# RWKV's inputs as a stream of their own in a three-mixer transformer block: separate generator, two input buffers, one PSUM bank, new interleaving tables

## The reference, cut to what matters

```python
y_a = hgrn2_mixer(a_q, a_ff, a_fb, a_i, lbs[l], ...) * jax.nn.silu(a_g)
y_b = retention_mixer(b_q, b_k, b_v, ...) * jax.nn.silu(b_g)
y_c = rwkv7_mixer(c_s, rwkv_mu[l], ...) * jax.nn.silu(c_g)
gates = jax.nn.sigmoid(merge.reshape(b, t, 3, D_MODEL))
mixed = (gates[:, :, 0] * (y_a @ w_branch_a[l]) + gates[:, :, 1] * (y_b @ w_branch_b[l])
         + gates[:, :, 2] * (y_c @ w_branch_c[l]))
x = x + (mixed @ w_out[l])
```

## Time and profile before

| What | Value |
|---|---|
| timed executions | 3178.53, 3178.54, 3192.47 us |
| the profiled execution | 3192.13 us, its span 3190.3 us |
| mean granted TensorE clock | 0.974 |
| TensorE busy | 3027.6 us, 95% of the span |
| VectorE / ScalarE / GpSimd busy | 52% / 22% / 8% |
| DMA queues, share of 16 engines | 33.2% weights, 3.3% the inverse's traffic |
| mixers of layer 0 | 31 to 1015.3 us |
| mixers of layer 1 | 1052 to 2031.6 us |

### The profile page before, as it was taken

One profiled execution on the slowest core, in us unless ns is written; L12 is line 12 of the kernel. 1 busy time (PEld: TensorE's weight loads), 2 busy tenths in 40 slices (PEclk: granted clock), 3 DMA queues, 4 the chain that ended last, 5 costly groups with the idle time before them and its releaser, 6 DMA issues.

```text
span 3190.3 us, 45074 instructions
## 1 busy us (share of the span) xinstructions
PE 3027.6 (95%) x18944; PEld 2516.2 (79%) x18944; DVE 1655.0 (52%) x3430; ACT 686.4 (22%) x1327; POOL 260.1 (8%) x326
## 2 busy tenths in 40 slices
PE   8989998889999998999799999899999999999999
PEld 7878877778887787888687888698677959866794
DVE  3556645456221464664645531176325757646575
ACT  3223423233110232342324211110111001013100
POOL 1201212012000020221102100000000000000000
PEclk9989989999999999999899999999999999999999
DMA  5323332233334332323223433445344544532453
GB/s 215 108 75 121 91 95 102 63 109 116 114 96 162 132 109 69 128 87 98 92 94 91 135 115 112 154 151 169 123 152 146 169 164 158 171 130 107 146 172 119
DMA packets 153753, 395.55 MB, mean 124 GB/s; under 512 B 90288, under 2 KB 106800, under 8 KB 109648
## 3 DMA queue, kind: packets, MB, share of 16 engines
q1 hardware_dynamic: 51376, 367.94, 33.2%
q10 hardware_dynamic: 100608, 19.93, 3.3%
q0 software_dynamic: 1568, 4.79, 0.4%
HBM read 380.04 MB, written 12.59 MB: 123 GB/s over the span
## 4 chain that ended last, share of the span: by engine, by line
PE 85%; DVE 7%; DMA 4%; ACT 1%; issue 1%; ACTq 1%; POOL 0%; DVEq 0%; SPq 0%
PE bank L414 27%; PE bank L1943 17%; PE bank L1961 7%; PE bank L431 6%; PE bank L1766 6%; PE bank L1829 3%; PE bank L1369 2%; PE bank L1972 1%; DMA rw_ex<-xT_scratch 1%; PE bank L749 1%; DMA xT_scratch<-rw_bm 1%; PE bank L768 1%; DVE rw_ex L680 1%; PE bank L916 1%; PE bank L1652 1%
## 5 line engine op out<-in xcount | busy, mean ns | idle before, releaser
L414 PE MATMUL bank<-h_features,weight_ring 128*128 128x256 f32 x4192 | 969.5, 388 | 9.9 <-DMA weight_ring<-in_w_in 4.9
L414 PEld LDWEIGHTS bank<-h_features,weight_ring 128*128 128x128 f32 x4192 | 799.4, 194 | 125.0 <-issue 5.1
L431 PE MATMUL bank<-weight_ring,h_features 128*128 128x256 f32 (+1 forms) x896 | 205.3, 379 | 0.6 <-ACT rt_qk L1670 0.6
L431 PEld LDWEIGHTS bank<-weight_ring,h_features 128*128 128x128 f32 x896 | 164.1, 190 | 24.8 <-issue 2.3
L1943 PE MATMUL bank<-h_features,weight_ring 128*128 128x128 f32 x1408 | 172.0, 275 | 6.1 <-DVE h_features L527 6.1
L1943 PEld LDWEIGHTS bank<-h_features,weight_ring 128*128 128x128 f32 x1408 | 164.3, 192 | 6.9 <-DVE h_features L527 6.9
L2014 ACT COPY mem_normed<-bank 128x128 f32<-128x128 f32 x88 | 23.5, 267 | 481.7 <-PE bank L1943 481.7
L1766 PE MATMUL bank<-y_features,weight_ring 128*128 128x256 f32 x512 | 120.7, 386 | 0.0
L1766 PEld LDWEIGHTS bank<-y_features,weight_ring 128*128 128x128 f32 x512 | 96.1, 192 | 13.4 <-issue 0.7
L2099 DVE TENSOR_TENSOR mem_normed<-mem_normed,bank 128x256 f32<-128x256 f32 x88 | 37.1, 421 | 130.8 <-PE bank L1943 130.8
L1943 PE MATMUL bank<-h_features,y_hgrn_features 128*128 128x128 f32 x704 | 93.0, 275 | 0.0
(11 more groups left out here) (544 smaller groups left out, 4925.1 us busy)
## 6 DMA issues: line engine op xcount, KB each, us to landing
weight_ring<-in_w_in SPq DMA_DIRECT2D x146, 1024.0 KB, 4.9
weight_ring<-in_f00w SPq DMA_DIRECT2D x33, 1024.0 KB, 4.8
weight_ring<-in_f01w SPq DMA_DIRECT2D x33, 1024.0 KB, 4.9
weight_ring<-in_f10w SPq DMA_DIRECT2D x33, 1024.0 KB, 4.9
weight_ring<-in_f11w SPq DMA_DIRECT2D x33, 1024.0 KB, 4.8
weight_ring<-in_w_b SPq DMA_DIRECT2D x16, 1024.0 KB, 4.9
weight_ring<-in_w_out SPq DMA_DIRECT2D x16, 1024.0 KB, 4.9
weight_ring<-in_conv_in SPq DMA_DIRECT2D x10, 1024.0 KB, 4.9
```

The source lines that it names most:

```text
L414: m = e.matmul(bank[:, j, :], w[:, k, j * P:(j + 1) * P], x[:, k, :], start=k == 0, stop=k == kt - 1, skip_group_check=True)
L431: m = e.matmul(bank[:, t * n:(t + 1) * n], x[:, k, t * P:(t + 1) * P], w[:, k, :], start=k == 0, stop=k == kt - 1, skip_group_check=True)
```

## The change

Five things change together.

1. RWKV's inputs (`c_r, c_k, c_v, c_g`, the `kk` norm, the transposes of `v`, the gate) leave the generators `rwkv_*` and become generators `rwkv_inputs_*`, a fourth letter P in the strings. `r, k, v, kk, vt` exist twice, so P of quarter q waits only for the end of quarter q - 2.
2. RWKV's four banks are divided: bank 3 alone for P, bank 0 for `rhs`, banks 1 and 2 for the rest of RWKV.
3. The gates of all three mixers are kept where the mixer's output will stand (`g.yc3`, `g.ya3`, `g.yT3`); `finish_dve` computes in another tile and multiplies into it. This frees three gate tiles.
4. The semaphore of the inverse is divided: one pair for the inverse (`x`), one for its transpose (`xT`), and the first doubling waits for `x` alone.
5. All the interleaving strings of the mixers are new, and equal for both layers.

```diff
 ("mixers0", "tensor"):
-    "H2 R20 H2 R5 H11 R4 H R6 H6 B6 H B3 R H2 R5 B R2 H2 R B R B R2 H2 R4 B2 R2 B R2 H2 R B R B R2 H2 R6 B3 "
+    "R P4 R4 H P4 H2 P4 H2 P5 H P H P H5 P H P4 H3 R2 P R2 P R2 P R4 P H6 B P4 B R H R3 P R2 P R2 P R P2 R H2 "
 ("mixers0", "sync"):
-    "H R4 H4 B6 H5 R4 B6 H5 B5 R4 B H B H B H B H B H B3 R4 B4 H2 B H B2 H B H B H B H2 B R8 ",
+    "P H P2 H P H2 P2 H B P2 B P B4 H4 B H P B P2 B4 P H5 B5 P B P3 B6 H2 B H2 B4 H B8 H9 R9 ",
...
-    R.r, R.k, R.v, R.kk, R.bonus = (R(n, *for_t) for n in ("r", "k", "v", "kk", "bonus"))
-    R.vt, R.o = R("vt", TT, 2 * P), R("o", TT, 2 * P)
-    R.gate = R("gate", *for_t)
+    R.inputs = [[R(f"{n}{i}", *for_t) for n in ("r", "k", "v", "kk")] + [R(f"vt{i}", TT, 2 * P)] for i in range(2)]
...
-    R.prod, R.x, R.xT = (... for z in (R.sig, R.bm, R.ex))
+    R.prod, R.x, R.xT = (... for z in (R.sig, R.ex, R.bm))
...
         if lv == BLOCK:
-            e.wait_ge(g.rw_inverse_sem, 64 * ((4 * l + q) * 2 + d + 1))
+            e.wait_ge(g.rw_x_sem, 32 * ((4 * l + q) * 2 + d + 1))
...
+            e.wait_ge(g.rw_xT_sem, 32 * ((4 * l + q) * 2 + d + 1))
...
+def rwkv_inputs_pe(e, g, l, q):
+    S = g.ri
+    _, _, v, _, vt = g.R.inputs[q % 2]
+    for name in ("c_r", "c_k", "c_v", "c_g"):
+        yield from features_pe(e, g, S, g.hT3, f"{name}{q}", l)
+    yield
+    bank = pairs(g.banks.take(S, "kkn", l, q))
+    ...
+def rwkv_inputs_act(e, g, l, q):
+    ...
+    if q >= 2:
+        e.wait_ge(*g.rw.dve.at("end", l, q - 2))
+    elif l:
+        e.wait_ge(*g.rw.dve.at("merged", l - 1, 3))
...
-    bank = g.banks.take(S, "rhs", *W)
+    bank = g.banks.take(g.rh, "rhs", *W)
...
-        e.tensor_tensor(y, y, gate[:, n0:n0 + 2, :], ALU.mult)
+        e.tensor_tensor(y, z, y, ALU.mult)
...
-        self.rw, self.hg = Stream(self, "rwkv", (0, 1, 2, 3)), Stream(self, "hgrn", (4, 5))
+        self.rw, self.hg = Stream(self, "rwkv", (1, 2)), Stream(self, "hgrn", (4, 5))
+        self.rh = Stream(self, "rwkv_rhs", (0,))
+        self.ri = Stream(self, "rwkv_inputs", (3,))
```

More of the change, by code:

```diff
@@ L771, in doublings_pe, with rwkv_inputs_sp @@
         yield
-def rwkv_sp(e, g, l):
+def rwkv_inputs_sp(e, g, l, q):
+    for name in ("c_r", "c_k", "c_v", "c_g"):
+        w_in_load(e, g, l, f"{name}{q}")
+        yield
+def rwkv_inputs_pe(e, g, l, q):
+    S = g.ri
+    _, _, v, _, vt = g.R.inputs[q % 2]
+    for name in ("c_r", "c_k", "c_v", "c_g"):
+        yield from features_pe(e, g, S, g.hT3, f"{name}{q}", l)
+    yield
+    bank = pairs(g.banks.take(S, "kkn", l, q))
+    for free in g.banks.free("kkn", l, q):
+        e.wait_ge(*free)
+    e.wait_ge(*S.dve.at("kk2", l, q))
+    for j in range(2):
+        m = e.matmul(bank[:, j, :], g.const("block_ones"), view(flat(vt), (2, T))[:, j, :], start=True, stop=True,
+                     skip_group_check=True)
+    m.then_inc(*S.pe.up("kkn", l, q))
+    for t in range(TT):
+        yield
+        if t == 0:
+            e.wait_ge(*S.dve.at(f"c_v{q}", l))
+        bank = g.banks.take(S, "vt", l, q, t)
+        for free in g.banks.free("vt", l, q, t):
+            e.wait_ge(*free)
+        for n in range(2):
+            m = e.transpose(bank[:, n * P:(n + 1) * P], v[:, n, t * P:(t + 1) * P], g.const("eye"))
+        m.then_inc(*S.pe.up("vt", l, q, t))
+    yield
@@ new lines, in rwkv_inputs_act @@
+def rwkv_inputs_act(e, g, l, q):
+    S = g.ri
+    pe, dve, act = S.pe, S.dve, S.act
+    r, k, v, _, vt = g.R.inputs[q % 2]
+    yield
+    if q >= 2:
+        e.wait_ge(*g.rw.dve.at("end", l, q - 2))
+    elif l:
+        e.wait_ge(*g.rw.dve.at("merged", l - 1, 3))
+    if q == 0:
+        e.wait_ge(*g.st.dve.at("mu", l))
+    for name, out, tile0 in (("c_r", r, 0), ("c_k", k, 8), ("c_v", v, 16)):
+        shifted_act(e, g, S, out, tile0 + 2 * q, f"{name}{q}", l)
+        yield
+    e.wait_ge(*pe.at(f"c_g{q}", l))
+    e.activation(g.yc3[:, 2 * q:2 * q + 2, :], pairs(g.banks.get(f"c_g{q}", l)), ACT.Sigmoid).then_inc(
+        *act.up(f"c_g{q}", l))
+    yield
+    e.wait_ge(*dve.at("kkv", l, q))
+    e.activation(vt, vt, ACT.Sqrt).then_inc(*act.up("kks", l, q))
+    for t in range(TT):
+        yield
+        e.wait_ge(*pe.at("vt", l, q, t))
+        e.wait_ge(*dve.at("kk", l, q))
+        e.copy(vt[:, t, :], g.banks.get("vt", l, q, t)[:, 0:2 * P]).then_inc(*act.up("vt", l, q, t))
+        g.banks.empty(act, "vt", l, q, t)
+    yield
@@ new lines, in rwkv_inputs_dve @@
+def rwkv_inputs_dve(e, g, l, q):
+    S = g.ri
+    pe, dve, act = S.pe, S.dve, S.act
+    r, k, v, kk, vt = g.R.inputs[q % 2]
+    norm = view(flat(vt), (2, T))
+    for name, out, tile0 in (("c_r", r, 0), ("c_k", k, 8), ("c_v", v, 16)):
+        yield
+        shifted_dve(e, g, S, out, tile0 + 2 * q, l, f"{name}{q}", l)
+        if name == "c_k":
+            yield
+            e.wait_ge(*dve.now())
+            for n in range(2):
+                z = e.tensor_scalar(kk[:, n, :], k[:, n, :], g.col(f"k_k{l}", 2 * q + n), None, ALU.mult)
+            z.then_inc(*dve.up())
+            e.wait_ge(*dve.now())
+            e.tensor_tensor(norm, kk, kk, ALU.mult).then_inc(*dve.up("kk2", l, q))
+    yield
+    gate = g.yc3[:, 2 * q:2 * q + 2, :]
+    e.wait_ge(*act.at(f"c_g{q}", l))
+    e.tensor_tensor(gate, gate, pairs(g.banks.get(f"c_g{q}", l)), ALU.mult).then_inc(*dve.up(f"c_g{q}", l))
+    g.banks.empty(dve, f"c_g{q}", l)
+    yield
+    e.wait_ge(*pe.at("kkn", l, q))
+    e.tensor_scalar(norm, pairs(g.banks.get("kkn", l, q)), 1.0, 1e-12, ALU.mult, ALU.add).then_inc(
+        *dve.up("kkv", l, q))
+    g.banks.empty(dve, "kkn", l, q)
+    yield
+    e.wait_ge(*act.at("kks", l, q))
+    e.reciprocal(norm, norm).then_inc(*dve.up())
+    e.wait_ge(*dve.now())
+    e.tensor_tensor(kk, kk, norm, ALU.mult).then_inc(*dve.up("kk", l, q))
+    yield
@@ L775, in rwkv_sp, with quarters @@
+def quarters(program, e, g, l):
     for q in range(4):
-        for name in ("c_r", "c_k", "c_v", "c_g"):
-            w_in_load(e, g, l, f"{name}{q}")
-            yield
+        yield from program(e, g, l, q)
 def rwkv_pe(e, g, l):
@@ L785, in rwkv_pe @@
     for q in range(4):
-        for name in ("c_r", "c_k", "c_v", "c_g"):
-            yield from features_pe(e, g, S, g.hT3, f"{name}{q}", l)
[L789 to L792, removed]
-            bank = g.banks.take(S, "vt", l, q, t)
-            for free in g.banks.free("vt", l, q, t):
-                e.wait_ge(*free)
-            for n in range(2):
-                m = e.transpose(bank[:, n * P:(n + 1) * P], R.v[:, n, t * P:(t + 1) * P], eye)
-            m.then_inc(*pe.up("vt", l, q, t))
-        yield
-        yield
-        bank = pairs(g.banks.take(S, "kkn", l, q))
-        for free in g.banks.free("kkn", l, q):
-            e.wait_ge(*free)
-        e.wait_ge(*dve.at("kk2", l, q))
-        for j in range(2):
-            m = e.matmul(bank[:, j, :], ones, R.ex[:, j, :], start=True, stop=True, skip_group_check=True)
-        m.then_inc(*pe.up("kkn", l, q))
+        _, _, _, _, vt = R.inputs[q % 2]
         for d in range(2):
@@ L1109, in rwkv_dve @@
     for q in range(4):
[L1110 to L1131 removed]
+        r, k, v_, kk, _ = R.inputs[q % 2]
         for d in range(2):
@@ L1268, in center_dve, with finish_dve @@
     yield
-def finish_dve(e, g, S, branch, yT, n_tiles, t0, gain, shift, bonus, gate, l, q):
+def finish_dve(e, g, S, yT, tmp, n_tiles, t0, gain, shift, bonus, l, q):
     dve = S.dve
@@ L1659, in retention_act @@
-def retention_act(e, g, l):
+    for name in ("b_q", "b_k"):
+        yield from features_pe(e, g, S, g.hT3, f"{name}{q}", l)
+    for s in range(2):
+        yield
+        bank = pairs(g.banks.take(S, "rot", l, q, s))
+        for free in g.banks.free("rot", l, q, s):
+            e.wait_ge(*free)
+        e.wait_ge(*act.at(("b_q", "b_k")[s], l, q))
+        for j in range(2):
+            m = e.matmul(bank[:, j, :], g.const("rot"), (B.q, B.k)[s][:, j, :], start=True, stop=True,
+                         skip_group_check=True)
+        m.then_inc(*pe.up("rot", l, q, s))
+        yield from tokens_pe(e, g, S, g.hT3, f"b_v{q}{s}", l)
@@ new lines, in retention_pe @@
+    for s in range(2):
+        yield from features_pe(e, g, S, g.hT3, f"b_g{q}{s}", l)
+    for h in range(2):
+        yield
+        bank = pairs(g.banks.take(S, "score", l, q, h))
+        for free in g.banks.free("score", l, q, h):
+            e.wait_ge(*free)
+        e.wait_ge(*dve.at("rot", l, q, 1))
+        for j in range(TT):
+            m = e.matmul(bank[:, j, :], B.k[:, h, j * P:(j + 1) * P], B.q[:, h, :], start=True, stop=True,
+                         skip_group_check=True)
+        m.then_inc(*pe.up("score", l, q, h))
+        yield
+        bank = g.banks.take(S, "mix", l, q, h).rearrange("p (t v) -> p t v", t=TT)
+        for free in g.banks.free("mix", l, q, h):
+            e.wait_ge(*free)
+        e.wait_ge(*dve.at("score", l, q, h))
+        e.wait_ge(*act.at(f"b_v{q}1", l))
+        for t in range(TT):
+            for j in range(TT):
```

(15 more changed lines are left out.)

323 lines of the change are left out of this document (120 added, 203 removed), and 96 rows, old and new, of the table ORDER.

## The result

The changed kernel takes 3091.1 us (median of four; 3085.3 to 3099.1), the kernel before, timed beside it, 3180.8 us. The ratio is 0.973, its 95% interval 0.970 to 0.976. The forecast was 3089, with a range of 3040 to 3145. The profiled execution took 3096.9 us, its span is 3095.1.

The account below looks back on a forecast made before the run. TensorE, busy 95%, bounds the kernel; only its mixers' idle time (111.0 us) and lower clock can be won. Idle 48 + 9 + 15 - 5 - 4 = 63 plus clock 27, together 90 off 3178.5, gives 3089; range 3040 to 3145.

Parts of the forecast that it names:

- HGRN: TensorE's waits at HGRN's finish, last mask and scale products: 55.8 us, of which 48 saved by cover, bounds 35 and 54.
- The inverse: TensorE's waits for loads of RWKV's block inverse: 18.8 us, 9 saved, bounds 0 and 17; need 28 to 32, cover 26 to 31.
- Ring, kk norm, bonus: TensorE's small waits for weight ring, kk norm and bonus: of some 19 us, 15 saved, bounds 8 and 18.
- P's bank: TensorE waiting for DVE's shift to read P's single bank: 5 us added for both layers, bounds 0 and 30.
- Score banks: RWKV's scores with two banks where they had four: about 1 us in a few of 16 units, 4 us added.
- Table loads: ScalarE's 25 added loads, 32 us, mostly paid beside other work; if all in TensorE's chains, 3121, chance 0.03.
- The clock: TensorE's lower clock in the mixers, real cost put at 47 us, follows the waits: 27 us saved.
- A: Rival: mixer waits move rather than go; about 40 us of idle saved, nothing of the clock: 3139, chance 0.20.
- B: Rival: nearly all mixer idle goes, 10 us per layer stay; 122 us saved, 3057, at the outside 3030; chance 0.16.
- C: Rival: slower, TensorE waits at P's single bank, 56 turns; 3256 at 3 us per turn, 3211 at 2.2; chance 0.07.
- D: Rival: cover does not matter, the streams' ends only meet elsewhere and the layer's time stays: 3178, chance 0.05.
- my case: Likeliest case: mixer waits mostly covered, 90 us saved, 3089 (3075 to 3120), chance 0.52.

Follow-up runs that it names:

- the old order: Changed kernel's structure with the orders of the kernel before: 3344.6 us, 1.052 of the kernel before; the same with two banks for P: 3239.2 us, 1.018.
- the run made for it: Changed kernel with the square root of the kk norm replaced by a plain copy, 14 table loads fewer: 3085.6 us, 0.970 of the kernel before.
- the control: Changed kernel run again, unedited, on the chip of the runs beside it: 3082.5 us, 0.970 of the kernel before.
- the loads held: Changed kernel with four weight loads per layer waiting on SyncE until the inverse has landed: 3049.4 us, 0.959; same edit in the kernel before: 3151.7 us, 0.992.

## Why the prediction was right, and where it was not

*HGRN: 48 us saved forecast, 52.6 came.* Right, and for the reason given. The same waits return with the old order (51.7 us), and return in part when the cover alone is taken away (24.6 us at six finishes). The chain, said to need 5.6 us, costs 4.1 in the mean when uncovered (up to 6.3), with its norm ahead of RWKV's work. The 2 us set aside for quarter 1 did not come.

*The inverse: 9 saved forecast, none came* (18.8 to 19.1). This is the step that failed. It read "need 28 to 32 us, cover 26 to 31" and took the need as the inverse's own, from landings of 2.5 and 3.6 us. Those medians of the kernel before hid what the other queue does, and they did not carry over: the stores' became 5.0 and 5.4 under the new order. The need grows with the weight chunks that move beside the transfers, up to 10.5 us and more for a load that takes 3.2 alone. The division was priced at about 1 us a unit; it was worth some 30 us in all, but only by making good part of this. I had looked at SyncE for the ring's sake alone, whether a chunk comes too late, and not for what its burst hits. The evidence stood in the kernel before too, in stores of up to 6.2 and loads of up to 7.1 us within the mixers.

*Ring, kk norm, bonus: 15 forecast.* None of the three has a row now. Over the run they had come to 4.9, 4.1 and 7.0, which is 16.0.

*P's bank: 5 forecast, 0.6 came.* Its price per turn was right to a tenth (3.07 us), and that the new order hides those 24 turns was right too, but for the 0.6.

*Score banks: 4 forecast, about 2 came.* The waits for L1222 at L910 and L923 sum to 3.0, as L848's did, and the products' busy time is 81.8 us where it was 80.0. But with the products side by side they cost 58.7, clock included, a sum I had not bounded: no rival held it.

*The low-rank weights: 0 forecast, 2.4 at L895. Table loads: 0 forecast,* none seen in the run made for it. ScalarE grew by 34.0 us (25 loads of 1.28 are 32), and that growth belongs to the order: with the old one its page counts 1327 instructions, as before. By the Trainium skill, "ScalarE: Activation LUTs", section "What ACT_TABLE_LOAD costs", a switch costs 2.66 us; by that figure 25 loads that all stand in TensorE's chains would have brought this case to 3155, an estimate. This trace does not agree: with 14 loads fewer ScalarE's busy time fell by 1.32 us each.

*Idle in all: 63 forecast, 70.0 in the mixers, 72.9 in the run.* Too little at HGRN, the small waits and the bank, too much at the inverse.

*The clock: 27 forecast.* 22.3 us of busy time went in the first profile and 36.2 in the control's. The forecast lies between, but both are taken from one execution of the kernel before, 11 us above its median. By the medians the gain was 89.7 us (91.8 beside the control); less the idle time, 72.9 and 76.4, that leaves 15 to 17 for the clock. This is an estimate, which takes the idle time of the profiled executions for that of the others; by it 27 was some 10 too much. That the clock follows the waits was right: the stages read 0.98 and 0.99 for 0.95 and 0.97, and every run that moved the idle time by more than 10 us moved busy time the same way (18.9 and 11.1 with the loads held; 29.2 and 16.5 at the finish), though not in proportion: the second bank for P took 75.4 us of idle time away and in the profiles only 3.6 of busy time. Of the eleven stretches at the lower clock that the changed kernel still has before the second block, four begin right behind an L752 that had waited for the inverse, and none of these four is left with the loads held. The windows around L752's wait in unit 1, of the changed kernel and of the one with the loads held, columns as in the earlier trace rows, have the clock third from the end: 0.77 with the wait, 1.00 without.

```profile
210.00:230.00 20.00, 17.15 (x180) 14.85 (x179) 6.48 (x13) 9.31 (x14) 0.43 (x1) 0.77 0.32 81
```

```profile
209.00:229.00 20.00, 18.67 (x239) 16.20 (x238) 7.03 (x15) 9.43 (x15) 1.63 (x2) 1.00 0.39 133
```

Not every fall has this cause. In the window 390 to 410 us the clock is at 0.83 in both runs; the waits in front of that fall are two of 0.95 and 0.93 us at the scores (L910).

*The rivals.* A (waits move, 3139) fell, though its words on the inverse, a need that exceeds its cover, were true. B (nearly all goes, 3057) was wrong for this kernel and is what it becomes with the loads held: 3049, with 7.5 and 11.1 us of idle time in the two stages. C fell with this order; its price of a turn came with the old one, in 24 turns and not in 56. D fell. Of the signs named for my case the short waits at the finish and the scale products and the empty row of the ring appeared. Four missed, the first three on the good side: the idle time of the two stages was 41.0 us where near 48 was said, layer 0's stage took 927 us where 935 to 945 was, layer 1's clock was 0.99 where 0.97 to 0.98 was, and the inverse's waits of 1 to 3 us were up to 4.1.

Forecast and result (3089, 3091) are closer than the steps, and that closeness is luck: 9 us too much at the inverse stood against some 19 too little elsewhere, and the 10 that this left over were about made up by the clock, which gave less than its 27 by either reckoning (22.3 in that profile, 15 to 17 by the medians).

## What to carry to other kernels

When a small transfer is on the path, look at what the other DMA queues issue between its issue and its landing, in each instance and not by the median. Here a queue that had waited 27.8 us for a slot then sent four chunks within 9.3 us. Where the ring has lead to spare, try one wait on that queue for the small transfer to land: here it was worth 33 us under the new order and 28 under the old one. Banks and order are one decision: under the old order a bank less cost P its full read time at each of 24 turns (3.07 us a turn), and under the new one, which puts work in front of the turns, 0.6 us in all.

## What the runs showed of the hardware

- A load of 128 KB in packets under 512 B takes 3.2 us alone, 4.6 to 6.2 beside one or two chunks of 1 MB, and 10.5 to 11.3 beside four, which themselves land in 7.1 to 8.0 (all medians of a place in the changed kernel, but for the 3.2 of the run with the loads held). The Trainium skill, "DMA: Bandwidth & Descriptors", section "Queues, rings and completion order", says that each DMA engine takes packets from its queues in turn; the landings fit that, but no view here shows the turns. Which share of it is packet size and which the bytes ahead, no run here separates.
- The issue was slowed as well: the two loads of the transpose took ScalarE's queue 5.00 us beside the four chunks (at 329.35 in the changed kernel) and 1.3 with the chunks held back.
- Two executions of the same program differed by 14 us of TensorE's busy time at nearly equal idle time (89.8 and 86.3), with the mean clock at 0.986 and 0.992.
- A mean duration can mix two clocks: of 256 score products with a mean of 509 ns, 150 took 403 at full clock and 106 took 659 where the lower clock was granted. The unit shown above at full clock had short waits between its products as the slow one had.
